# Issuing a transformer layer's expert rows in groups of four: Pool's gather order in a Trainium2 kernel

## The reference

```python
u_e = expert_down[expert]
act = gelu(einsum('chkd,cd->chk', u_e, xc))
v_e = expert_up[expert]
out = einsum('chk,chkd->cd', (g * act).astype(xc.dtype), v_e)
```

## Time and profile before

| | |
|---|---|
| median of 3 runs | 1822.85 us (1820.48 to 1825.32) |
| profiled execution, own time | 1827.09 us |
| its span, first to last instruction | 1825.3 us |
| mean granted PE clock | 0.952 |
| PE busy | 1478.4 us, 81% |
| DVE busy | 1116.1 us, 61% |
| Pool busy | 984.7 us, 54% |
| ACT busy | 437.8 us, 24% |
| DMA, whole span | 604.97 MB, 331 GB/s |

### The profile page before, as it was taken

One profiled execution on the slowest core, in us unless ns is written; L12 is line 12 of the kernel. 1 busy time (PEld: TensorE's weight loads), 2 busy tenths in 40 slices (PEclk: granted clock), 3 DMA queues, 4 the chain that ended last, 5 costly groups with the idle time before them and its releaser, 6 DMA issues.

```text
span 1825.3 us, 14454 instructions
## 1 busy us (share of the span) xinstructions
PE 1478.4 (81%) x4072; PEld 688.0 (38%) x4072; DVE 1116.1 (61%) x2733; ACT 437.8 (24%) x1119; POOL 984.7 (54%) x1054
## 2 busy tenths in 40 slices
PE   6999988798898997776986988877788776776785
PEld 5444557434443453222432433322344222222232
DVE  5550367776676766667565676656455674665664
ACT  3111345322221322122222222221221221122121
POOL 1000000666666666666566666666676666666663
PEclk8999999899999999999899999999898999988889
DMA  9965402999999999999899999999999999999996
GB/s 308 380 231 116 162 4 49 341 346 361 360 365 383 407 374 367 374 363 370 310 364 406 386 362 364 376 360 378 362 371 363 357 372 385 359 362 372 372 361 257
DMA packets 190618, 604.97 MB, mean 331 GB/s; under 512 B 30898, under 2 KB 31306, under 8 KB 190380
## 3 DMA queue, kind: packets, MB, share of 16 engines
q0 software_dynamic: 147456, 536.94, 77.6%
q1 hardware_dynamic: 42027, 64.30, 10.6%
q10 hardware_dynamic: 1056, 2.82, 0.5%
HBM read 600.64 MB, written 3.34 MB: 331 GB/s over the span
## 4 chain that ended last, share of the span: by engine, by line
PE 42%; POOL 15%; issue 13%; DMA 13%; DVE 10%; another core or an unknown queue 5%; ACT 2%; SPq 0%; DVEq 0%; POOLq 0%; ACTq 0%
PE pair L939 23%; POOL big L681 10%; PE pair L691 9%; DMA big<-in_expert_up,expert_idx 7%; POOL region_v L681 4%; DVE big L1528 3%; PE pair L753 3%; DMA region_v<-in_expert_up,expert_idx 3%; PE pair L779 2%; DMA big<-in_expert_down,expert_idx 2%; PE pair L718 2%; DMA region_v<-in_expert_down,expert_idx 1%; DVE region_v L1528 1%; PE pair L798 1%
## 5 line engine op out<-in xcount | busy, mean ns | idle before, releaser
L939 PE MATMUL pair<-big 128*128 128x512 f32 x1460 | 734.5, 630 | 211.5 <-DMA big<-in_expert_up,expert_idx 94.3
L1528 DVE CUSTOM_DVE_ANT_0 big<-big,pair 128x1024 f32<-128x1024 f32 x363 | 440.5, 1219 | 241.4 <-DMA big<-in_expert_down,expert_idx 166.8
L939 PEld LDWEIGHTS pair<-big 128*128 128x128 f32 x1460 | 269.4, 197 | 592.8 <-issue 564.5
L681 POOL DMA_INDIRECT big<-in_expert_up,expert_idx x365 | 346.2, 948 | 239.3 <-issue 85.3
L681 POOL DMA_INDIRECT big<-in_expert_down,expert_idx x363 | 344.7, 949 | 122.7 <-issue 101.7
L939 PE MATMUL pair<-region_v,big 128*128 128x512 f32 x588 | 295.1, 624 | 76.1 <-DMA region_v<-in_expert_up,expert_idx 33.4
L1163 ACT ACTIVATE big<-ident,big 128x128 f32<-128x128 f32 x512 | 163.6, 390 | 371.3 <-issue 205.8
L1528 DVE CUSTOM_DVE_ANT_0 region_v<-region_v,pair 128x1024 f32<-128x1024 f32 x149 | 181.6, 1220 | 98.9 <-DMA region_v<-in_expert_down,expert_idx 72.1
L681 POOL DMA_INDIRECT region_v<-in_expert_up,expert_idx x147 | 139.3, 948 | 107.7 <-PE pair L939 44.2
L939 PEld LDWEIGHTS pair<-region_v,big 128*128 128x128 f32 x588 | 107.0, 196 | 220.9 <-issue 205.3
L681 POOL DMA_INDIRECT region_v<-in_expert_down,expert_idx x149 | 142.2, 955 | 52.6 <-issue 39.3
(11 more groups left out here) (156 smaller groups left out, 1080.5 us busy)
## 6 DMA issues: line engine op xcount, KB each, us to landing
big<-in_w_ada SPq DMA_DIRECT2D x8, 2048.0 KB, 22.3
big<-in_w_in SPq DMA_DIRECT2D x5, 2048.0 KB, 13.1
big<-in_w_ada SPq DMA_DIRECT2D x16, 512.0 KB, 11.9
big<-in_w_query SPq DMA_DIRECT2D x4, 2048.0 KB
big<-in_expert_up,expert_idx POOLq DMA_INDIRECT x365
big<-in_expert_down,expert_idx POOLq DMA_INDIRECT x363
big<-in_w_out SPq DMA_DIRECT2D x2, 2048.0 KB
big<-na_scr SPq DMA_DIRECT2D x24, 128.0 KB, 4.4
```

Source lines behind the costliest of these rows:

```text
L681: nc.gpsimd.indirect_dma_start(places[place], None, (expert_down if kind == "down" else expert_up)[0], bass.IndirectOffsetOnAxis(expert_id ...
L939: last = nc.tensor.matmul(pair[t % 2][:, s * HALF:(s + 1) * HALF], diag[:, j, :], places[place][:, s * HALF:(s + 1) * HALF], start=(h == 0 ...
L1528: v.tensor_tensor_reduce(out=places[place], in0=places[place], in1=u_cur[:, :], scale=1.0, scalar=0.0, op0=ALU.mult, op1=ALU.add, accum_ou ...
```

## The change

`gather_order` is written anew. It starts with the same eight down rows; then four up rows and four down rows go out in turn. `UP_LAG`, `FIRST_UP`, `CLOSE_FROM` and `CLOSE_LAG` have no use any more. Nothing else in the code differs; the table of places follows from the list.

```diff
 def gather_order():
 
-    order, ups = [], 0
-    for at in range(SETS):
-        order.append(("down", at))
-        for _ in range(2):
-            if at >= FIRST_UP and ups <= at - (UP_LAG if at < CLOSE_FROM else CLOSE_LAG):
-                order.append(("up", ups))
-                ups += 1
-    order += [("up", at) for at in range(ups, SETS)]
-    return order
+    order = [("down", at) for at in range(QUARTER)]
+    for first in range(QUARTER, SETS, QUARTER):
+        order += [("down", first + i) for i in range(QUARTER)]
+        order += [("up", first - QUARTER + i) for i in range(QUARTER)]
+    return order + [("up", SETS - QUARTER + i) for i in range(QUARTER)]
```

## The result

| | before | after |
|---|---|---|
| median | 1824.09 us (1820.48 to 1829.96, 4 runs) | 1864.67 us (1862.05 to 1867.43, 4 runs) |
| profiled execution, own time | 1827.09 us | 1867.43 us |
| its span | 1825.3 us | 1865.6 us |
| mean granted PE clock | 0.952 | 0.913 |

The ratio is 1.0207, with a 95% interval of 1.0182 to 1.0232: the change makes the kernel slower, by 41 us by the medians and 40.3 us between the two profiled executions. The forecast was 1833 us.

The account below looks back on a forecast made before the run. Pool's gather issue was taken as the bound from about 341 to 1806 us, its waits costing nearly their length. 6 + 2 + 0 + 2 = 10 us gave 1837 us profiled, 1833 us median; 8-in-10 range 1802 to 1864 us.

Parts of the forecast that it names:

- Slower: Whole kernel: the change makes it slower, by the forecast's own path or through PE's clock; chance 0.51.
- (b): Weights: down row 4q+4 leads up row 4q by 4 gathers, not 7; 2 us, ends 0 and 27 us.
- (a): Eight-place stretch: the fourth up row holds its place past a round; 6 us of 0 to 25 us.
- The later stretches: With 12 to 20 places, rounds outlast the holding of places, so spare places cover it; 0 us.
- the no-change rival: Whole kernel: holding times stay under a round and Pool waits as often; 1823 us, chance 0.27.
- (c): PE's clock: a low-clock first row per group takes 1.45 us more, held by the 3.7 us gap; 0 us.
- (d): The end: eight up rows in a run finish later, partly offset by Pool's waits; 2 us, ends -3 and +4.
- Faster: Pool waits less: With 12 and 20 places, fewer waits for up_done, PE's count of finished up rows; 30 us, 1793 us, chance 0.22.
- The clock rival: Third stretch: low PE clock lasts through bursts, one group in five gives +38 us; 1863 us, chance 0.10.

Follow-up runs that it names:

- lag 5: Kernel before, one and one, with up rows 5 sets behind instead of 7; 1738.36 us against 1705.85, +32.5 us.
- both cures: Changed kernel with nine down rows first, then fours, and ACT emptying PE's banks ahead of its wait for the weights; 1834.47 us, +8.8 us over before.
- the run made to test it: Kernel before with seven more, already satisfied, PE waits ahead of each up row; 1705.00 us against 1705.85.

## Why the prediction was right on the sign and short on the size

**Direction and place: right.** Slower had 0.51, and what was named as the sign of it came: fewer than 101 gathers in the first stretch (88), with waits before up rows, and the last stretch near 1.44 us a gather (1.450). The stretch between did not keep it: 279/185 = 1.508 us for 1.438, since the eight-place part now ends at about 530 us and not 495. PE's matmuls do come in fours: of its 66 bursts between 770 and 1800 us (parted by more than 1 us of idle time) 36 hold four up rows, with a median gap of 3.1 us. The last issue to the last matmul is 12.1 us, not 10. A sign named for being wrong came too, a clock under 0.9 after 770 us (0.89), though only some 4 us were lost there in all.

**The sum: 10 us for 41.** Its terms against what was measured:

- **(b) is the step that failed.** It saw rightly that the down row 4q+4 leads by 4 gathers instead of 7, but it priced the late weights only as "the up row waits in its place, up to 3.8 us more than now", in about 7 quarters, and took 2 us since the calm chain of 1.8 us fits in 5.1 us. Two things were missed. The down row is queued on Pool behind up rows that wait for a place, so it goes out later by that wait (5.33, 7.04 us) while PE works off the rows it has; a lead of 4 x 1.28 us over the next up row says nothing of PE's lead over the dot. And ACT empties PE's banks behind the diagonals, so late weights stop PE itself, in work that has nothing to do with this up row. An edit of ACT's queue took 33 of 56.5 us away, lag 5 alone cost 32.5 us; with the bounds of 0 and 27 us even the upper one was too low on that chip. On the slow chip no single cure was run with the fours, so how much of the 41 us is (b)'s there stays open; both cures together left 8.8 us.
- **(a) was mis-sized.** I took 6 us of 0 to 25. With the loop cut, Pool was still 21 us behind at gather 117 on the fast chip: near the upper end, not a quarter of it. Holding times were worked out at the mean pace of 2.63 us an up row against a mean round; but the groups with query steps come together, and there three of the four rows of a group wait, 1.7 to 2.1 us each. How much of it is (a)'s on the slow chip was not measured alone; with both cures 7 us stayed where the change had 32.
- **The later stretches, 0: nearly right.** "0, covered by the spare places" failed in one place. Between gathers 192 and 384 the change loses 6 us in the first comparison and 14 us on the fast chip, and on the latter PE again waits for ACT's evacuation: between 790 and 900 us, 5.9 + 2.3 us in the change on the fast chip against 2.9 us in before. In the first comparison the gathers' pace after 770 us is about the same, as the no-change rival had it for this part.
- **(c) The clock, 0: right.** It fell after 770 us from 0.94 to 0.89, and Pool was 31 us behind at gather 320 (about 820 us) and 35 us at the last. The rule on HAM oscillation that the prediction weighed (the Trainium skill, TensorE: Matmul & The Clock Gate) describes bursts that start cold after a DMA wait, and puts a price on each. The traces agree on the lower clock and show no price in the late stretch of the fast chip: 0.95 against 1.00 from 950 to 1640 us, with 536 gathers in both. In the eight-place stretch the low clock follows the idle times of the loop; there it can add to the loss, 3.62 us for an up row instead of 1.88, and how much was not measured alone.
- **(d) The end, +2: +4.1 us**, 0.1 us outside its ends of -3 and +4. Eight up rows took 13.97/8 = 1.75 us each, where 1.83 was forecast; the 2 us that waits were to give back do not show: from gather 900 to the last the change stays 35 us behind.

**The rivals.** "Nothing changes" held for the work after gather 384 alone. "Faster: Pool waits less" was to decide once the waits for up_done fall under 200 us; from 341 to 1800 us those put down to PE or to "remote" were 226.8 us and are 230.7 us. The clock rival gave 1863 us, near the result, by a mechanism that did not act: its price stood in the third stretch, where some 4 us were lost. The range ended at 1864 us and the median is 1864.67 us. That the result lies at its end is luck: the coupling that took most of the time is in none of the terms that the range was made from.

## What to carry to other kernels

When an order of issue is changed on a queue whose entries wait for places, measure each lead in time and with the waits of what stands in between, not in entries: a producer queued behind a waiting consumer closes a loop. And follow a late value past its own consumer, through everything that stands behind it on each in-order queue; here the evacuation of another product's banks stood behind the weights and did the greater harm. Moving such work ahead of the wait cost nothing with the turns and gave 33 us back with the fours; 24 us stayed, so it makes the kernel less sensitive to the order, not indifferent to it.

## What the hardware showed that was not expected

**Pool's stops belong to the chip, not to the program.** In the first trace Pool waits 47 times between 341 and 1800 us for something that the profile calls "remote", for 103.4 us in all:

```profile
POOL big L681 <- remote: 73.5, 33, 4.4
...
POOL region_v L681 <- remote: 29.9, 14, 3.6
```

The same program on the fast chip has no such row; all of Pool's waits from 341 us on, with those for issue left out, are these:

```profile
POOL big L681 <- PE pair L939: 51.6, 114, 2.8
POOL region_v L681 <- PE pair L939: 33.1, 52, 6.0
POOL big L681 <- DVE expert_idx L1321: 15.0, 8, 2.6
POOL big L681 <- DVE big L1528: 12.5, 33, 1.2
POOL region_v L681 <- DVE big L1528: 7.9, 17, 1.5
POOL region_v L681 <- DVE expert_idx L1321: 4.8, 2, 2.5
POOL big L681 <- PE pair L787: 0.3, 1, 0.3
```

and its window from 1450 to 1460 us, to set beside the earlier trace rows, moves 409 GB/s where the first moved 268:

```profile
1450.00:1460.00 10.00, 7.58 (x17) 2.56 (x16) 5.93 (x12) 1.48 (x5) 6.56 (x8) 1.00 1.02 409
```

There 409 GB/s last nearly through the whole of the late stretches, and before takes 1707 us instead of 1824: 118 us, 6.5%, for one and the same kernel. The stops are in all six traces at the slow pace and in none of the eight of the fast chip.

In a stop PE has long been done. The gather at 1453.04 us takes the place of up row 374, by the table of places. Counted in fours from the first (and the rows from 0), that row's matmuls are the second half of this line and end at 1431.21 + 3.60 = 1434.81 us, 18.2 us before Pool goes on:

```profile
1431.21 3.60 PE L939 MATMUL pair<-big 128*128 128x512 f32 x8
```

Done so for every wait of Pool for an up row, the trace splits its idle time (above the 0.30 us of issue) in two: what passed up to 0.27 us after the last matmul of that row, and what passed later. In the trace of before on the fast chip the first part is 28 us and the second 0. In the first trace the first part is 14 us and the second 181 us, with delays of up to 22 us. So some 180 of the 225.7 us that the prediction read as waiting for PE were waits for a count of work already done, and the label "<-PE" hides this as well as "remote" does. Why the count comes late on that chip was not found. Counted in the first trace, half of the steps from one stop of over 1.5 us to the next hold 45 to 56 matmuls of PE, with a median of 51; in gathers they are 14 to 23 and in time 20 to 33 us, which scatters more. The other five traces of that pace have medians of 48 to 52 matmuls. That is in favour of the prediction's reading that the stops go with PE's stream; the run made to test it fell on the fast chip, so it is not shown.

409 GB/s over 690 us also settle the rule weighed in the prediction, that one core's limit is about 358 GB/s (the Trainium skill, DMA: Bandwidth & Descriptors): it does not bind one core working alone. The Trainium skill's Perfetto Trace Analysis (Roofline) says so too: about 120% of that figure is the practical ceiling of a single core. Here 409/358 is 114%. The Trainium skill's advice to run matmuls back to back in batches (Perfetto Trace Analysis, Matmul Optimizations) rests on the engine's power scaling with its use. Here the order in fours did batch them, with gaps between the batches, and the granted clock after 770 us was lower with it than with turns, 0.89 against 0.94; the time, though, was lost by the loop and not by the batches as such.

**The price of an order depends on the chip.** The change costs 41 us where before takes 1824 us and 56.5 us where it takes 1707 us, and the two traces of each pair tell where the difference lies. At the slow pace, in the sense of the split above, Pool's waits for rows that PE had not finished grow from 14 to 68 us, but those for counts that come late shrink from 181 to some 159 us: the loop's waits take the place of some of the stops. On the fast chip there are no stops to replace. Whether this is all of the 15 us was not tested.
